# Expert passes of a two-layer trunk: the next expert's token rows fetched by an indirect DMA and turned, in place of one-hot products

## The reference, cut to what matters

```
logits = (t @ w_router).astype(jnp.float32)
top_val, top_idx = lax.top_k(logits, TOP_K)
top_w = jax.nn.softmax(top_val, axis=-1)
combine = jnp.sum(jax.nn.one_hot(top_idx, N_EXPERTS) * top_w[..., None], axis=1)
for e in range(N_EXPERTS):
    out = out + combine[:, e:e + 1] * _swiglu(t, wg[e], wu[e], wd[e])
```

## Time and profile before

| | us |
|---|---|
| median of 3 runs | 1502.22 (1500.8 to 1505.39) |
| the profiled execution | 1506.64 |
| its span, first to last instruction | 1504.9 |

### The profile page before, as it was taken

The page is one execution under the profiler, slowest core; times in us unless marked ns, Lnnn a source line. Parts: engine busy times, 40 slices in busy tenths (PEclk is TensorE's granted clock), DMA queues, the critical chain, the costliest instruction groups (busy, mean ns, idle before and its releaser), DMA issues.

```text
span 1504.9 us, 18806 instructions
## 1 busy us (share of the span) xinstructions
PE 1450.9 (96%) x7173; PEld 1189.9 (79%) x7173; DVE 1267.0 (84%) x1067; ACT 912.6 (61%) x810; POOL 14.2 (1%) x55
## 2 busy tenths in 40 slices
PE   4988899998989999999999999999999999999998
PEld 1774898996775888888888888888888888888886
DVE  3479668776777899899899899989989989999997
ACT  2072534432263677677677677767767767776774
POOL 1000000000000000000000000000000000000000
PEclk9999899999999899999999999999999999999999
DMA  8945569767727599999999899999999999989990
GB/s 347 346 196 185 215 223 370 280 244 280 289 86 279 202 368 368 336 361 373 336 350 381 327 357 362 345 368 354 375 341 350 372 333 356 377 320 360 380 340 28
DMA packets 191290, 468.68 MB, mean 311 GB/s; under 512 B 8502, under 2 KB 31252, under 8 KB 187156
## 3 DMA queue, kind: packets, MB, share of 16 engines
q1 hardware_dynamic: 186736, 451.17, 81.4%
q0 software_dynamic: 2288, 16.79, 2.8%
q10 hardware_dynamic: 2228, 0.22, 0.1%
HBM read 467.10 MB, written 1.05 MB: 311 GB/s over the span
## 4 chain that ended last, share of the span: by engine, by line
PE 90%; DVE 6%; ACT 2%; issue 1%; DMA 1%; ACTq 0%; DVEq 0%
PE ps L959 20%; PE ps L961 20%; PE ps L960 20%; PE ps L648 4%; PE ps L827 2%; PE ps L828 2%; PE ps L829 2%; PE ps L918 2%; PE ps L794 2%; PE ps L641 2%; PE ps L998 2%; PE ps L836 1%; PE ps L837 1%; PE ps L835 1%; PE ps L575 1%
## 5 line engine op out<-in xcount | busy, mean ns | idle before, releaser
L1815 DVE TENSOR_TENSOR split_r<-arena,split_r 128x2048 fp32r<-128x2048 f32 x339 | 770.7, 2289 | 59.3 <-ACT split_r L1259 58.3
L1259 ACT ACTIVATE split_r<-arena 128x2048 fp32r<-128x2048 f32 x338 | 648.7, 1921 | 118.5 <-PE ps L961 118.5
L959 PE MATMUL ps<-split_r,tokens_r 128*128 128x512 f32 x1280 | 504.2, 394 | 0.2 <-DVE split_r L1815 0.2
L961 PE MATMUL ps<-split_r,tokens_r 128*128 128x512 f32 x1280 | 499.1, 390 | 0.0
L960 PE MATMUL ps<-split_r,tokens_r 128*128 128x512 f32 x1280 | 498.7, 390 | 0.0
L961 PEld LDWEIGHTS ps<-split_r,tokens_r 128*128 128x128 f32 x1280 | 240.3, 188 | 50.5
L959 PEld LDWEIGHTS ps<-split_r,tokens_r 128*128 128x128 f32 x1280 | 240.4, 188 | 49.0 <-DVE split_r L1815 0.6
L960 PEld LDWEIGHTS ps<-split_r,tokens_r 128*128 128x128 f32 x1280 | 240.5, 188 | 48.3
L827 PE MATMUL ps<-tokens_r,split_r 128*128 128x256 f32 x352 | 99.8, 283 | 5.7 <-DVE hT_r L1701 5.0
L828 PE MATMUL ps<-hT_r,split_r 128*128 128x256 f32 x352 | 99.8, 284 | 0.0
L829 PE MATMUL ps<-tokens_r,split_r 128*128 128x256 f32 x352 | 99.7, 283 | 0.0
(11 more groups left out here) (320 smaller groups left out, 1425.4 us busy)
## 6 DMA issues: line engine op xcount, KB each, us to landing
arena<-in_moe_w_gate SPq DMA_DIRECT2D x57, 2048.0 KB, 9.7
arena<-in_moe_w_up SPq DMA_DIRECT2D x57, 2048.0 KB, 9.2
arena<-in_moe_w_down SPq DMA_DIRECT2D x56, 2048.0 KB, 9.4
arena<-in_w_ada POOLq DMA_DIRECT2D x10, 1536.0 KB, 11.0
arena<-in_w_ada SPq DMA_DIRECT2D x14, 1024.0 KB, 12.7
arena<-in_ffn_w_gate SPq DMA_DIRECT2D x11, 1024.0 KB, 6.9
arena<-in_ffn_w_up SPq DMA_DIRECT2D x11, 1024.0 KB, 12.5
arena<-in_ffn_w_down SPq DMA_DIRECT2D x11, 1024.0 KB, 14.8
```

What stands on the lines that cost most here:

```text
L959: mm(out_, xh, h, start=first, stop=False, skip_group_check=True)
L961: return mm(out_, xl, h, start=False, stop=last_, skip_group_check=True)
L1259: A(wh[:, j % SPLITS, :], piece_half(j), ACT.Copy).then_inc(sem("w_hi"), 1)
L1815: v.tensor_tensor(wl[:, j % SPLITS, :], piece_half(j), wh[:, j % SPLITS, :].bitcast(F32), ALU.subtract).then_inc(sem("w_lo"), 1)
```

## The change

- Once, ahead of the loop, GpSimd writes the 256 rows of `hnat` to a DRAM tensor `h_rows` (1 MB), and an iota puts each token's number beside its weight in `w_row`, which takes the place of `w_tok`.
- In each pass, after j = 26 (ROWS_AFTER), `slot_rows(p + 1)` on TensorE multiplies `sel` with the token numbers (two fp32 matmuls of one column into bank 7), and VectorE at j = 28 casts the result to `slot_row`, 128 row numbers.
- GpSimd runs a loop of its own: it waits for `slot_row` and issues an indirect DMA of 128 rows of 4 KB from `h_rows` into `hrow`, which lies on the first half of `hnat`.
- After j = 37, `turn_rows(p + 1)` turns `hrow` by 8 transposes, in place of `gather(p + 1)`. `gather(0)` stays.
- The transposes of chunk 5, which write bank 7, wait for `slot_row` as well.
- Some semaphores are merged (`g2` into `pad`, `rank_ps` into `lg_ps`, `w_dif` into `chosen`, `ffn_gate` into `gate_row`), with counts to match.

```diff
+        slot_row = sb("slot_row", 1, U32)
+        h_rows = nc.dram_tensor("h_rows", (SEQ, D), F32, kind="Internal").ap()
-        w_tok = rs[:, 32:34]
-        w_slot = rs[:, 34:35]
+        w_row = rs[:, 32:36].rearrange("p (t c) -> p t c", t=NT)
+        w_slot = rs[:, 36:37]
+        hrow = part(F, 0, D)
...
+        ROWS_AFTER = 2 * pieces.index(("d", 3))
...
+            g.iota(w_row[:, :, 1:2], pattern=[[P, NT], [1, 1]], base=0, channel_multiplier=1,
+                   allow_small_or_imprecise_dtypes=True).then_inc(sem("no_outputs"), 1)
+            pool.wait_ge(sem("no_outputs"), 3)
             g.memset(mark[:, 3:4], 0.0).then_inc(sem("y_sb"), 1)
+            pool.wait_ge(sem("hnat"), 2)
+            g.dma_start(h_rows.rearrange("(t p) d -> p t d", p=P), hnat).then_inc(sem("late_bias_in"), 16)
+            pool.wait_ge(sem("meta"), 1)
+            pool.wait_ge(sem("late_bias_in"), 48)
+            passes = pool.value_load(meta[0:1, COUNT:COUNT + 1], min_val=NE, max_val=2 * NE)
+            with pool.Fori(0, passes) as p:
+                pool.wait_ge(sem("slot_row"), p + 1)
+                pool.value_load(meta[0:1, bass.ds(p, 1)], min_val=0, max_val=NE - 1)
+                g.indirect_dma_start(hrow, None, h_rows, bass.IndirectOffsetOnAxis(ap=slot_row[:, 0:1], axis=0))\
+                    .then_inc(sem("hrow"), 16)
...
+            def slot_rows(p):
+
+                pe.wait_ge(sem("sel"), p + 1)
+                for t in range(NT):
+                    last = mm(ps[:, 7, 0:1], sel[:, t, :], w_row[:, t, 1:2], start=(t == 0), stop=(t == NT - 1))
+                last.then_inc(sem("row_ps"), 1)
+
+            def turn_rows(p):
+
+                pe.wait_ge(sem("hrow"), 16 * p)
+                for k in range(KD):
+                    last = tr(ps[:, 2 + k // 4, (k % 4) * P:(k % 4 + 1) * P], hrow[:, k * P:(k + 1) * P], ident[:, :])
+                    if k % 4 == 3:
+                        last.then_inc(sem("gath_ps"), 1)
...
+                    if j == ROWS_AFTER:
+                        slot_rows(p + 1)
                     if j == GATHER_AFTER:
-                        gather(p + 1)
+                        turn_rows(p + 1)
                     if j in turn_after:
                         c = turn_after[j]
                         pe.wait_ge(sem("e_hid"), p * ECHUNKS + c + 1)
                         if c == 1:
                             pe.wait_ge(sem("swT"), p + 1)
+                        if c == 5:
+                            pe.wait_ge(sem("slot_row"), p + 1)
...
+                    if j == ROWS_AFTER + 2:
+                        dve.wait_ge(sem("row_ps"), p + 1)
+                        v.tensor_copy(slot_row[:, 0:1], ps[:, 7, 0:1]).then_inc(sem("slot_row"), 1)
```

More of the change, by code:

```diff
@@ L519, in _ @@
                     pool.wait_ge(sem("setup"), 2)
-                g.memset(wbd[:, 0, :, :], 0.0).then_inc(sem("g2"), 1)
-                g.memset(wbd[:, 1, :, :], 0.0).then_inc(sem("g2"), 1)
+                g.memset(wbd[:, 0, :, :], 0.0).then_inc(sem("pad"), 1)
+                g.memset(wbd[:, 1, :, :], 0.0).then_inc(sem("pad"), 1)
                 g.memset(xp[:, :, 0:TAPS - 1], 0.0).then_inc(sem("pad"), 1)
-                pool.wait_ge(sem("g2"), 2 * (l + 1))
-                pool.wait_ge(sem("pad"), l + 1)
+                pool.wait_ge(sem("pad"), 3 * (l + 1))
                 g.memset(mark[:, 0:1], 0.0).then_inc(sem("wbd_zero"), 1)
@@ L545, in _ @@
             g.memset(ynat, 0.0).then_inc(sem("no_outputs"), 1)
-            pool.wait_ge(sem("no_outputs"), 2)
+            g.iota(w_row[:, :, 1:2], pattern=[[P, NT], [1, 1]], base=0, channel_multiplier=1,
+                   allow_small_or_imprecise_dtypes=True).then_inc(sem("no_outputs"), 1)
+            pool.wait_ge(sem("no_outputs"), 3)
             g.memset(mark[:, 3:4], 0.0).then_inc(sem("y_sb"), 1)
+            pool.wait_ge(sem("hnat"), 2)
[8 more added lines that the diff above has]
+                    .then_inc(sem("hrow"), 16)
         @block.tensor
@@ L900, in experts @@
                 mm(ps[:, 2, 2 * NE:3 * NE], ones[:, :], rs[:, NE:2 * NE], start=False, stop=True, skip_group_check=True)\
-                    .then_inc(sem("rank_ps"), 1)
+                    .then_inc(sem("lg_ps"), 1)
                 pe.wait_ge(sem("hnat"), 2)
@@ L906, in experts @@
                 weights(0)
-                pe.wait_ge(sem("gate_row"), 1)
+                pe.wait_ge(sem("gate_row"), 2)
                 passes = pe.value_load(meta[0:1, COUNT:COUNT + 1], min_val=NE, max_val=2 * NE)
@@ L927, in weights @@
                 for t in range(NT):
-                    last = mm(ps[:, 7, NT * P:NT * P + 1], sel[:, t, :], w_tok[:, t:t + 1], start=(t == 0),
+                    last = mm(ps[:, 7, NT * P:NT * P + 1], sel[:, t, :], w_row[:, t, 0:1], start=(t == 0),
                               stop=(t == NT - 1))
@@ L1104, in mixer @@
                 root(3 * NT, 40)
-                act.wait_ge(sem("pad"), l + 1)
+                act.wait_ge(sem("pad"), 3 * (l + 1))
                 act.wait_ge(sem("rec_ps"), 2 * l + 1)
@@ L1233, in dense @@
                 act.wait_ge(sem("grow_ps"), 2)
-                A(gacc, bank2(2), ACT.Copy).then_inc(sem("ffn_gate"), 1)
+                A(gacc, bank2(2), ACT.Copy).then_inc(sem("gate_row"), 1)
             def experts():
@@ L1243, in experts @@
                 A(gate_row, bank2(0), ACT.Copy).then_inc(sem("gate_row"), 1)
-                act.wait_ge(sem("w_dif"), 1)
+                act.wait_ge(sem("chosen"), 2)
                 A(st[:, 8:10], st[:, 8:10], ACT.Tanh, scale=0.5).then_inc(sem("w_exp"), 1)
@@ L1728, in dense @@
                 modulation(2)
-                dve.wait_ge(sem("ffn_gate"), 1)
+                dve.wait_ge(sem("gate_row"), 1)
                 down_update(0, 0)
@@ L1758, in experts @@
                 v.tensor_tensor(st[:, 8:10].unsqueeze(2), top[:, :, 1:2], top[:, :, 0:1], ALU.subtract)\
-                    .then_inc(sem("w_dif"), 1)
-                dve.wait_ge(sem("rank_ps"), 1)
+                    .then_inc(sem("chosen"), 1)
+                dve.wait_ge(sem("lg_ps"), NT + 1)
                 dve.wait_ge(sem("chosen"), 1)
@@ L1797, in experts @@
                 link(v.tensor_tensor(wts, one[:, :, 0, :], one[:, :, 1, :], ALU.add))
-                v.tensor_copy(w_tok.unsqueeze(2), wts[:, :, 0:1]).then_inc(sem("meta"), 1)
+                v.tensor_copy(w_row[:, :, 0:1], wts[:, :, 0:1]).then_inc(sem("meta"), 1)
                 low_h(0)
@@ L1834, in select @@
                     v.tensor_scalar(sel[:, t, :], slots, posm[:, t, bass.ds(e, 1)], None, ALU.is_equal)
-                v.tensor_copy(w_tok.unsqueeze(2), wts[:, :, bass.ds(e, 1)]).then_inc(sem("sel"), 1)
+                v.tensor_copy(w_row[:, :, 0:1], wts[:, :, bass.ds(e, 1)]).then_inc(sem("sel"), 1)
             def add(p, t):
```

## The result

| | before | changed |
|---|---|---|
| median of 4 runs, us | 1501.84 (1500.8 to 1505.39) | 1487.44 (1485.18 to 1489.52) |
| the profiled execution | 1506.64 | 1489.52 |
| its span | 1504.9 | 1487.8 |
| one pass, gather to gather or turn to turn | 123.94 | 121.72 |

The ratio is 0.9888, with a 95% interval of 0.987 to 0.9906: 14 to 20 us faster. The forecast was 1484.1, 18.1 us faster, with a range of 1480 to 1496.

A forecast was written before the change was run, and what follows sets the result against it. TensorE, busy for all of each 123.94 us pass, was taken to bound the loop; 3.58 - 0.87 - 0.45 = 2.26 us over 8 passes gives 18.1 us off 1502.22, so 1484.1, with a range of 1480 to 1496.

The forecast's parts named there:

- the sum: Per pass on TensorE: gather's 3.58 us less 0.87 and 0.45 added, 2.26 us saved, 18.1 us over 8 passes.
- transposes: Eight 128x128 fp32 transposes on TensorE replacing the gather: 0.87 us a pass, bounds 0.79 to 0.90.
- row numbers: slot_rows on TensorE, four records: 0.45 us a pass, or 0.37 without the slow first matmul behind it.
- The span: Profiled execution's span, 1504.9 us, was to fall by 18.1 us to 1486.8.
- The cover: Added work outside TensorE stays hidden at no cost; the cast uncovered would cost 1.4 us in all.
- the added wait: Chunk 5's transposes waiting for slot_row, five half steps after the cast: costs nothing.
- The bound for the fetch: GpSimd's fetch lands like its plain 1.5 MB transfers, 7.9 to 15.2 us, within 22.7 us available.
- Rival A: DMA transfers become the bound at 355 GB/s; 6 to 12 us paid, time 1490 to 1496; chance 0.10.
- the stock of landed weights: Weights landed ahead of ScalarE's reading would absorb 19 to 25 us of the 31 us lost to slow transfers.
- Rival B: Fetched rows land too late and turn_rows waits; landing 28 us after the cast gives 1526; chance 0.08.
- Rival C: VectorE's crowded stretch behind the gather makes TensorE wait up to 2.26 us a pass, 1502; chance 0.05.
- the anchor: VectorE's gapless run starts at half 43's split, hanging on TensorE's half step 40; its near-zero slack doesn't fall.

The follow-up runs named there:

- e2: Changed kernel without the indirect fetch, GpSimd only setting one column and posting the semaphore; 1486.73 us, ratio to before 0.9891.
- e5: Changed kernel with the cast to slot_row, and so the fetch, 4 half steps later; 1486.8 us, ratio to before 0.9889.
- e7: Changed kernel plus two 1 MB DRAM-to-DRAM copies on GpSimd's queue in each pass; 1485.11 us, ratio to before 0.9874.
- e8: Changed kernel plus four 1 MB DRAM-to-DRAM copies on GpSimd's queue in each pass; 1498.42 us, ratio to before 0.9971.
- e12: Changed kernel with the next pass's turned tokens split one iteration earlier; 1488.19 us, ratio to before 0.9872.
- e1: Changed kernel with all it adds, but the gather's 16 one-hot products kept instead of the 8 transposes; 1509.0 us, ratio to before 1.0044.
- e6: Changed kernel with the row numbers after half step 34 and the cast at iteration 35, making the fetch late on purpose; 1548.01 us, ratio to before 1.0293.
- e4: Changed kernel with row numbers and slot weights formed in one pair of two-column products; 1486.56 us, ratio to before 0.989.

## Why the prediction was right

- **TensorE bounds the loop, and the sum.** 123.94 to 121.72 us a pass, 2.22 where 2.26 was forecast; transposes 0.88 for 0.87, row numbers 0.46 for 0.45. Right in each term. Of the 0.04 us between them 0.02 are in the two terms; a wait at half step 6, which grew from about 0.05 to 0.09, can be the rest.
- **The span.** It fell by 17.1 us, not 18.1. Seven passes from turn to turn give 15.5, the end behind the last turn another 2.8, and the start gave 1.2 back: the first turn begins at 610.77, the first gather in the loop began at 609.56. 0.46 of that are the row numbers. GpSimd's first job of the expert stage, ahead of all that the change adds but the merged semaphores, already began at 493.3 instead of 491.55. That is the spread between executions: in the traces of e2, e5, e7, e8 and e12, whose work up to there is the changed kernel's, the first turn begins between 604.9 and 609.8, and in the changed kernel at 610.6 by the same view. The median fell by less than the profile, 14.4 us, and 1487.44 lies just above the 1481 to 1487 that the prediction gave for its own sum; the ratio's interval (14 to 20) holds 18.1. The spread of the runs is 4 us, and nothing finer can be said of the total.
- **The cover.** The cast, the fetch, the write to DRAM and the added wait cost nothing, as forecast (e1, e2). The bound for the fetch taken from plain transfers of 1.5 MB (7.9 to 15.2 us) was the right neighbour: 8.1 to 11.0.
- **Rival A.** Ruled out by e7: 382 GB/s without loss; the stock of landed weights that the prediction counted on is seen at work in e8. The 358 GB/s of the Trainium skill ("DMA: Bandwidth & Descriptors", Specifications), by which the gain would have gone, doesn't hold for this core here, where one core runs: 366 GB/s over whole passes of the changed kernel and 391 in e8, 34 of them copies within DRAM.
- **Rival B.** Its price was too low. e6 shows the clock as a second cost of a wait; by its 1.4 us a pass, 28 us from the cast would have given some 11 us more than the 1526 stated, an estimate.
- **Rival C.** Off for this change, but by less than the prediction said. It put the anchor right (half 43's split, behind TensorE's half step 40) and took "its slack doesn't fall" from it. The rows show the anchor with 0.13 us of gap before, 0.09 after, and none in e4. The step that it lacked is to ask how far the anchor is from the next one.

## What to carry to other kernels

When the engine that bounds a loop is busy throughout, the price of a step is the distance of starts around it, and sums made so held to 0.04 us in 122. Before counting on the next saving, find the gap at the front of the neighbour's gapless run. In e4 that gap was all that could be won until the front moved, and moving work into an idle gap of the same engine did it where giving it to another engine made it worse. A pass measured inside one execution tells apart tenths of a us that medians of whole runs can't.

## What the runs showed of the hardware that I had not expected

- TensorE's granted clock fell to 0.50 during a wait of 6.4 us and stayed there for the next 2.7 us of work: the wait cost 7.8. It fell in every pass of e6, also in the last with its wait of 2.9 us.
- DMA engines that show 0.96 to 0.99 of busy share at 355 to 366 GB/s still took 382 GB/s without delay to TensorE, at a share of 1.02, and 390 to 392 over whole passes at 1.04. The share said little about the room left.
- An indirect fetch of 128 rows of 4 KB held GpSimd for 1.67 us (2.6 in e6) and landed in 5.0 to 11.0 us in e5 and the changed kernel, in passes that move 366 GB/s, no slower than the plain transfers of 1.5 MB (7.9 to 15.2).
- VectorE lost 1.4 us beside one GpSimd subtraction that read SBUF; with the indirect fetch beside it no split was longer than 2.295 us.
